# A two-layer hybrid diffusion backbone: output projection in pair steps, middle vectors in buffers of their own, gate pieces ahead of attention, y rests on VectorE

## What is computed

```python
for l in range(2):
    h = rmsnorm(x) * (1 + sc1) + sh1            # sc, sh, g come from silu(c) @ mod_w[l] + mod_b[l]
    ym = sigmoid(h @ w_mo) * head_norm(mlstm(h))          # 4 heads of 128, both directions
    ya = window_attention(rope(h @ w_aq), ...)            # 8 heads of 64, window 128, sink
    yr = silu(h @ w_rg) * head_norm(retention(h))         # 4 heads, values 256 wide, both directions
    y = (sigmoid(h @ w_gm) * (ym @ w_br_m) + sigmoid(h @ w_ga) * (ya @ w_br_a)
         + sigmoid(h @ w_gr) * (yr @ w_br_r)) @ w_out
    x = x + g1 * y
    h2 = rmsnorm(x) * (1 + sc2) + sh2
    x = x + g2 * conv_ffn(h2)                             # 2816 wide, gated, conv over 3 tokens
out = rmsnorm(x) * final_norm_w
```

## Time and profile before

| what | value |
|---|---|
| three runs | 3087.06, 3088.95, 3093.79 us; median 3088.95 us |
| the profiled execution's own time | 3092.63 us |
| its span from the first to the last instruction | 3090.8 us |
| TensorE busy | 2915.1 us, 94% of the span |
| granted TensorE clock, mean | 0.976 of full speed |
| VectorE, ScalarE, GpSimd busy | 37%, 32%, 39% |
| DMA | 249.8 MB, 81 GB/s over the span |

### The profile page before, as it was taken

One profiled execution on the slowest core, in us unless ns is written; L12 is line 12 of the kernel. 1 busy time (PEld: TensorE's weight loads), 2 busy tenths in 40 slices (PEclk: granted clock), 3 DMA queues, 4 the chain that ended last, 5 costly groups with the idle time before them and its releaser, 6 DMA issues. The chain is left out here.

```text
span 3090.8 us, 48199 instructions
## 1 busy us (share of the span) xinstructions
PE 2915.1 (94%) x19520; PEld 2586.9 (84%) x19520; DVE 1152.7 (37%) x2711; ACT 981.2 (32%) x1672; POOL 1216.5 (39%) x1078
## 2 busy tenths in 40 slices
PE   7999899999999997999999989989999989799998
PEld 5899878898888995888888779987898889788876
DVE  4545435423331023433333635424523320233345
ACT  4333225432322114322222333323532332332332
POOL 2333411153444423433443334341164455455554
PEclk9999999999999998999999999999999999899999
DMA  5111200022222125111111321120022322322222
GB/s 221 56 69 48 77 34 21 8 93 82 83 96 83 55 76 198 55 69 68 69 55 69 116 90 69 49 96 28 15 93 104 125 87 87 119 83 95 96 96 102
DMA packets 39385, 249.81 MB, mean 81 GB/s; under 512 B 4480, under 2 KB 4864, under 8 KB 13568
## 3 DMA queue, kind: packets, MB, share of 16 engines
q1 hardware_dynamic: 36288, 236.25, 21.5%
q10 hardware_dynamic: 2880, 10.49, 0.8%
HBM read 236.23 MB, written 10.49 MB: 80 GB/s over the span
## 5 line engine op out<-in xcount | busy, mean ns | idle before, releaser
L2090 POOL TENSOR_TENSOR w_rest<-raw,w_head 128x512 fp32r<-128x512 f32 (+1 forms) x642 | 842.0, 1344 | 991.8 <-ACT w_head L1193 982.0
L817 PE MATMUL psum_products<-w_head,h_head 128*128 128x256 f32 x2368 | 689.4, 291 | 0.0
L817 PE MATMUL psum_products<-w_rest,h_head 128*128 128x256 f32 x2368 | 666.2, 281 | 0.0
L817 PE MATMUL psum_products<-w_head,h_rest 128*128 128x256 f32 x2368 | 665.5, 281 | 0.0
L817 PE MATMUL psum_products<-h_head,w_head 128*128 128x512 f32 (+3 forms) x1696 | 600.1, 354 | 11.6 <-POOL w_rest L2090 8.6
L817 PE MATMUL psum_products<-h_head,w_rest 128*128 128x512 f32 (+3 forms) x1696 | 596.5, 352 | 0.0
L817 PE MATMUL psum_products<-h_rest,w_head 128*128 128x512 f32 (+3 forms) x1696 | 596.4, 352 | 0.0
L817 PEld LDWEIGHTS psum_products<-w_head,h_head 128*128 128x128 f32 x2368 | 454.0, 192 | 4.0 <-issue 1.4
L817 PEld LDWEIGHTS psum_products<-w_rest,h_head 128*128 128x128 f32 x2368 | 453.0, 191 | 1.3
L817 PEld LDWEIGHTS psum_products<-w_head,h_rest 128*128 128x128 f32 x2368 | 453.6, 192 | 0.0
L1193 ACT ACTIVATE w_head<-raw 128x2048 fp32r<-128x2048 f32 (+2 forms) x170 | 307.5, 1809 | 449.5 <-PE psum_products L817 392.7
(11 more groups left out here) (255 smaller groups left out, 3996.1 us busy)
## 6 DMA issues: line engine op xcount, KB each, us to landing
raw<-in_stream SPq DMA_DIRECT2D x192, 1024.0 KB, 4.8
raw<-in_stream SPq DMA_DIRECT2D x16, 512.0 KB, 3.3
residual<-stage ACTq DMA_DIRECT2D x16, 512.0 KB, 2.8
stage<-residual SPq DMA_DIRECT2D x14, 512.0 KB, 5.6
mods_b<-in_stream SPq DMA_DIRECT2D x5, 1024.0 KB, 24.1
mods_a<-in_stream SPq DMA_DIRECT2D x3, 1024.0 KB, 13.9
x_in<-in_x SPq DMA_DIRECT2D x4, 512.0 KB, 8.8
stage<-in_x SPq DMA_DIRECT2D x4, 512.0 KB, 5.9
```

What stands on the lines that cost most here:

```text
L817: return nc.tensor.matmul(o, a, b, start=start, stop=stop)
L2090: G.tensor_tensor(wl[:, s["sp"] % 2, a:b], place_of(s)[:, a:b], wh[:, s["sp"] % 2, a:b].bitcast(F32), ALU.subtract).then_inc(*ev.mark("poo ...
```

## The change

It has six parts.

1. **Output projection.** Of the four column blocks only 0 and 1 are done whole. Blocks 2 and 3 alternate pair by pair, and behind each such step but the first stands one tick of `norms`: (pair 0, block 2), (pair 0, block 3), tick 0, (pair 1, block 2), tick 1 and so on. The head of h is freed pair by pair (`h_free`) instead of with the whole slot (`w_free`).
2. **Middle vectors.** The eight vectors of layer 0's middle get four buffers of their own (`mods_mid`, in the arena over the MLP's rings), and stand behind the fifth tick: 6 pieces, tick 5, 6 pieces, tick 6, 4 pieces. SyncE issues their first four loads at the last `wout` block (`ahead = 6`).
3. **Gate pieces.** Four of the attention's gate pieces stand ahead of tick 0 of `attend`, behind the rotary steps; `attend` spreads four fewer.
4. **The end of the mLSTM.** In its last head two more vectors are taken: one more piece 0 behind each of the last ticks, and their pieces 1 behind `ysplit`.
5. **Retention.** Heads 2 and 3 take two vectors each instead of three.
6. **y rests.** The rest of yT in `ysplit` is made by VectorE instead of GpSimd.

```diff
@@ make_plan
+    def vectors(count, homes=False):
+
+        turn, mids = None, []
         for l, n in islice(modulation, count):
-            now = vector(l, n, cols("mod_w", l, n * COLS, splits=False))
+            s = cols("mod_w", l, n * COLS, splits=False, home=8 + len(mids) % 4 if homes else None)
+            if homes:
+                s["before"] = mids[-4] if len(mids) >= 4 else None
+                mids.append(s["n"])
+            now = vector(l, n, s)
...
             if hd + 1 == MH:
+                late = vectors(2)
+                pieces, fill = pieces + 2, chain(fill, islice(late, 2))
                 ticks("mtiles", count, fill, pieces, l=l, hd=hd, tiles=tiles)
                 continue
...
         step("ysplit", l=l, br="m", kt=4, tiles=tiles)
+        for _ in late:
+            pass
...
-        ticks("attend", AH * len(tiles) + 3, fill, 12 * len(pairs(ctx)), l=l,
+        for _ in islice(fill, 4):
+            pass
+        ticks("attend", AH * len(tiles) + 3, fill, 12 * len(pairs(ctx)) - 4, l=l,
...
-            more, last = vectors(3), len(tiles) + 1
-            more_now = 6 if hd + 1 < RH else 4
+            count_v = 3 if hd < 2 else 2
+            more, last = vectors(count_v), len(tiles) + 1
+            more_now = 2 * count_v if hd + 1 < RH else 2
...
-        for n in range(3):
+        for n in range(2):
             step("wout", cols("w_out", l, n * COLS), 3, l=l, gen=gen, n=n, ctx=ctx)
         step("affine", l=l, which=1)
-        wout, h_gen = cols("w_out", l, 3 * COLS), gen
+        wouts, h_gen = [cols("w_out", l, n * COLS) for n in (2, 3)], gen
...
-        for pair in pairs(ctx)[:-1]:
-            step("wout", wout, 1, l=l, gen=h_gen, n=3, ctx=ctx, pair=pair, part=pair, open=True)
-        ticks("norms", 2, stop=2, **mid)
-        step("wout", wout, 1, l=l, gen=h_gen, n=3, ctx=ctx, pair=2, part=2)
-        fill = vectors(2 * D // COLS) if ctx else iter(())
-        for k in range(2, len(tiles) + 2):
+        k = 0
+        for pair in pairs(ctx):
+            for i, n in enumerate((2, 3)):
+                step("wout", wouts[i], 1, l=l, gen=h_gen, n=n, ctx=ctx, pair=pair, part=pair,
+                     open=(pair, n) not in ((pairs(ctx)[0], 2), (2, 3)))
+                if pair != pairs(ctx)[0] or n == 3:
+                    step("norms", ticks=range(k, k + 1), **mid)
+                    k += 1
+        fill = vectors(2 * D // COLS, homes=True) if ctx else iter(())
+        for k in range(k, len(tiles) + 2):
+            for _ in islice(fill, 6 if k < len(tiles) + 1 else 4):
+                pass
             step("norms", ticks=range(k, k + 1), **mid)
-            for _ in islice(fill, 3):
-                pass
@@ backbone
+        home_mid = Region(8 * 1024 + 128)("mods_mid", [P, 4, SLOT])
...
                     ahead = 1 if kind == "split" else 3 if s["sp"] is not None else 2
+                    if kind == "wout" and st["n"] == 3 and st["ctx"]:
+                        ahead = 6
...
                             if use == "mid":
+                                act.wait_ge(*ev.at("h_free", st["l"], t // 2))
...
+                elif kind == "ysplit":
+                    for t in st["tiles"]:
+                        ts = slice(t * P, (t + 1) * P)
+                        dve.wait_ge(*ev.at("yh", l, st["br"], t))
+                        V.tensor_tensor(yl[:, 0:st["kt"], ts], yT[:, 0:st["kt"], ts],
+                                        yh[:, 0:st["kt"], ts].bitcast(F32), ALU.subtract).then_inc(
+                            *ev.mark("dve", "ysplit", l, st["br"], t))
```

More of the change, by code:

```diff
@@ L117, in slot @@
     def slot(l, blocks, kt=KD, splits=True, home=None):
-        s = dict(n=len(stream), l=l, blocks=blocks, kt=kt, cols=sum(b[1] for b in blocks[2]), sp=None, home=home)
+        s = dict(n=len(stream), l=l, blocks=blocks, kt=kt, cols=sum(b[1] for b in blocks[2]), sp=None, home=home,
+                 before=None)
         if home is None:
@@ L163, in vector @@
         return turn
-    def vectors(count):
-        turn = None
+    def vectors(count, homes=False):
+        turn, mids = None, []
         for l, n in islice(modulation, count):
-            now = vector(l, n, cols("mod_w", l, n * COLS, splits=False))
+            s = cols("mod_w", l, n * COLS, splits=False, home=8 + len(mids) % 4 if homes else None)
[3 more added lines that the diff above has]
+            now = vector(l, n, s)
             yield
@@ L651, in place_of @@
                 return raw[:, s["r"] % 2, 0:n]
+            if s["home"] >= 8:
+                return home_mid[:, s["home"] - 8, 0:n]
             return home_a[:, s["home"], 0:n] if s["home"] < 3 else home_b[:, s["home"] - 3, 0:n]
@@ L751, in load @@
                 s = STREAM[i]
-                if s["home"] is None and s["before"] is not None:
+                if s["before"] is not None:
                     sp.wait_ge(*ev.at("raw_free", s["before"]))
@@ L999, in _ @@
                     part_b(st, 0, COLS)
+                    if kind == "wout" and st["n"] == 3:
+                        ev.now["h_free", l, st["pair"]] = {"pe": ev.count["pe"]}
                 elif kind == "branch":
@@ L1246, in _ @@
                         if k >= 2 and use != "last":
-                            if k == 2 and st["h_slot"] is not None:
+                            t = st["tiles"][k - 2]
+                            if use == "mid":
+                                act.wait_ge(*ev.at("h_free", st["l"], t // 2))
+                            elif k == 2 and st["h_slot"] is not None:
                                 act.wait_ge(*ev.at("w_free", st["h_slot"]))
-                            t = st["tiles"][k - 2]
                             act.wait_ge(*ev.at("hf", st["gen"], k - 2))
```

7 lines of the change are left out of this document (removed).

## The result

| | before | after | ratio (95% interval) |
|---|---|---|---|
| median of the runs, first timing | 3088.38 us | 3039.59 us | 0.9831 (0.9805 to 0.9857) |
| the same two kernels, second timing | 3101.19 us | 3037.18 us | 0.9793 (0.9776 to 0.9811) |
| the same two kernels, third timing | 3098.98 us | 3043.63 us | 0.9822 (0.9798 to 0.9846) |
| span of the profiled executions | 3090.8 us | 3037.6, 3034.2, 3044.2 us | |

A forecast was written before the change was run, and what follows sets the result against it. TensorE, busy 94% of the span, was taken as the bound, with its waits and low clock. Six terms summed to 63.8 us: 3092.6 to 3028.8 profiled, 3025 for the median, range 3009 to 3050.

The forecast's parts named there:

- Term 1: Layer 0's middle: pair steps cover tick chains and vector slots come ahead; 87.0 to 63.3 us, 23.7 saved, bounds 20 to 30.
- Term 2: Layer 1's middle: the 5.41 wait goes, the 6.42 wait stays, only earlier; 5.5 us saved, bounds 3 and 8.
- Term 3: Four gate pieces ahead of attention fill 4.78 of waiting and restore 1.6 of clock; 12.8 us saved in two layers.
- Term 4: Retention's branch: y rests on VectorE remove waits of 3.50 and 4.08 and half clock; 11.0 us saved, bounds 5 and 13.
- the serial case: Retention's branch, at worst: y rests and weights' rest one behind the other, done 3.2 us early in layer 0, 0.4 in layer 1.
- Term 5: End of the mLSTM: shorter chain to the branch product, two added vectors hidden; 4.5 us saved, bounds 0 and 6.
- Term 6: Retention: four vectors fewer in two layers at 1.58 each; 6.3 us saved if hidden where they went, else 0.
- Attention shortened: Against the rival that attention's ticks are chains and do not shorten: 12.8 us lost, 3038; chance alone 0.13.
- The middle of layer 0 was not held up: Against the rival that GpSimd or vector slots hold it up: gain 12, not 23.7, 3037; chance 0.17, with loads held up.
- The slower case: Both middles: if a tick's chain exceeds its 5.65 step, TensorE waits at ten places at half clock; 3100 us, chance 0.03.
- No part failed to do what it says: Against the rival of vector loads late in SyncE's order: middle's 7.48 back, 15 us, 3040; chance 0.17, with middle held up.
- the waits for `xs` would fall from seven to two or three: Sign in the changed profile: that fall in TensorE's `xs` waits, none over 1 us in layer 0's pair-step ticks.

The follow-up runs named there:

- the other spread: Changed kernel with retention-head pieces dealt out two a tick until none is left, in place of evenly: 3033.16 us, ratio 0.9780 to the kernel before.
- mid_order_old: Changed kernel with both middles in the order before, the vectors still in buffers of their own: 3048.99 us, ratio 0.9859 to the kernel before.
- gates_in: Changed kernel with the four gate pieces put back among attention's ticks: 3055.21 us, ratio 0.9872 to the kernel before.
- Ret3: Changed kernel with three vectors in each retention head again and none added at the mLSTM's end: 3045.26 us, ratio 0.9813 to the kernel before.

## Why the prediction was right or wrong

Gains in the stretches, before (one trace) against the mean of the three traces of the changed kernel:

| term | forecast | found | by itself |
|---|---|---|---|
| 1. middle, layer 0 | 23.7 | 22.1 (on the mean of seven) | order 9.5, buffers 17.8 |
| 2. middle, layer 1 | 5.5 | 3.5 | order 0.8 |
| 3. attention | 12.8 | 8.0 + 9.3 = 17.3 | 15.1 (14.1 on twelve) |
| 4. y rests at the retention | 11.0 | 5.8 + 4.9 = 10.7 | 10.2 |
| 5. end of the mLSTM | 4.5 | 0.8 + 1.1 = 1.9 | |
| 6. retention heads 2, 3 | 6.3 | -1.1 + 0.0 (0.1 + 0.2 on ten) | 10 to 11 more with the other spread |
| sum | 63.8 | 54.4 | |

The spans differ by 52.1 (3090.8 against 3038.7 on the mean of three); in these three traces alone term 1 is 23.4 and the sum 55.7, so 3.6 us were lost elsewhere. The forecast's sum was too high by 9.4 in these stretches, and that is terms 5 and 6 above all (10.8 forecast, 0.8 found), then term 2 and term 1; that term 3 made up for 4.5 of it was luck. How near the size came is a matter of the timing too: the sum's 63.8 stands beside 48.8 at the first, and 64.0 and 55.4 at the others.

- **Term 1 was right** in its steps: 61.8, 62.2 and 66.8 us for 63.3, no wait over 1 us for `xs` at the pair steps, no slot waited for, and the one wait put down at 3.3, GpSimd with the first MLP slot's rests in hand, stands there as 3.40 (the last row below). It left out one that the new order brings in both layers, 1.53 ahead of block 3's first pair, whose weights' rest is not made yet. The group `const,vec` was misread: its 5.34 ran at clock 0.70 and not at half, and at full it takes 3.82, not 2.7, so that the 4.2 put down held by luck.

```profile
1128.07 0.38 PE L838 MATMUL psum_products<-w_head,h_head 128*128 128x256 f32 x1 [1.53 <-POOL w_rest L2122]
...
1168.56 0.75 PE L951 MATMUL psum_mixers<-const,xs 128*128 128x128 f32 x4 [3.40 <-ACT xs L1282]
```

- **Term 2 was too large.** The step that failed is "so this stays, only earlier". The 5.41 went and the 6.42 became 9.10. First, the 6.42 was not GpSimd's four pieces, as the forecast read it. Those ended at 2686.23, and GpSimd then waited 2.35 for the tick's squares; what held the tick was its sum, 2.35 long behind the last eviction, and an inverse root that took 1.40 beside VectorE's next sum:

```profile
2684.24 0.69 DVE L1663 TENSOR_TENSOR acc<-psum_products,gate_b 128x512 f32<-128x512 f32 x1 [5.99 <-PE psum_products L817]
2684.97 2.35 DVE L1625 TENSOR_TENSOR stage<-stage,acc 128x1024 f32<-128x1024 f32 x1
```

```profile
2688.59 0.19 POOL L2117 TENSOR_SCALAR small<-small 128x1 f32<-128x1 f32 x1 [2.35 <-ACT xs L1235]
2688.86 1.40 POOL L2120 TENSOR_TENSOR small<-small,const 128x1 f32<-128x1 f32 x1
```

In the changed kernel the statistic follows the four pieces by 0.08, so now they bound the tick. Second, they came hardly earlier: they began 28.6 us into the window before (2681.17 - 2652.6) and 27.2 after (2631.43 - 2604.2), while TensorE was done with the second tick's transposes 6.0 earlier (from the windows' starts, 32.5 and 26.5). The head of that slot stands behind the second tick in ScalarE's list, in both kernels, and that tick has a pair step more ahead of it now. The weight buffer was free by then: VectorE evicts the last product with block 2 from 2622.92 on, and ScalarE starts the head 6.5 later, without a wait, right behind the tick's `hf`:

```profile
2628.06 1.49 ACT L1293 ACTIVATE hf<-psum_mixers,aff 128x128 f32<-128x128 f32 x4
2629.43 1.92 ACT L1216 ACTIVATE w_head<-raw 128x2048 fp32r<-128x2048 f32 x1
```

All waits over 0.3 us of this stretch are 17.3 in mid_order_old and 15.8 in the changed kernel. Of the 3.5 found only that 0.8 is the order's. Mid_order_old has the order of before, and still takes 78.3 against its 81.0: the same 336 matmuls of the output projection took 38.3 us there and 39.8 before, both at clock 1.00, and the clock behind the same wait of 5.41 was 0.88 and 0.72. So the other 2.7 lies in the one trace of the kernel before, and is not a gain of the change.
- **Term 3 was too small** by 1.3 to 4.5, by which of its sizes one takes. The wait and the half clock are as summed: from the first product to the end of `attend` it is 7.4 shorter in layer 0, 5.65 + 1.6 being 7.25 (8.8 in layer 1). The late start was put at 0.9 and is 0.5 in layer 0. What was left out is the gate step ahead of the branch: in layer 0 it ran at clock 0.92 in 18.9 us before, and at 1.00 in 17.5 to 18.2 in the changed kernel. In gates_in it is back at 19.1 and 0.92, so in layer 0 it belongs to the pieces; in layer 1 gates_in ran it at 1.00 too.
- **Term 4 was right**, in its sum and in its margin: both waits went, 10.7 for 11.0. Of the serial case by which it was bounded the rows show the order, but not that the port made it. By the rule of the Trainium skill, "SBUF — State Buffer", section "Who interferes with whom", which made the two take turns, the trace agrees in layer 1 only in so far as they did not overlap, which the end of the weights' head explains as well; the contention itself is in the middle, where a sum beside GpSimd's rests took 2.17 and four rests 6.20, and 1.23 and 5.03 apart.
- **Term 5 was wrong in its chain and its clock**, not in its vectors. It put the chain to the branch at 1.2 shorter in layer 0 and 1.3 in layer 1, with 0.3 and 1.7 of clock behind. Ret3, without the two vectors, shows the y rests alone: the wait of 2.93 only fell to 2.31 in both layers, and the 4 us behind it ran at 0.62 and 0.60, where the kernel before had 1.00 and 0.57. So the chain gave 0.6, and no clock came back:

```profile
343.73 0.55 PE L834 MATMUL psum_products<-w_head,y_head 128*128 128x256 f32 x1 [2.31 <-DVE y_rest L1946]
```

The two vectors are hidden as forecast: 62.3 and 44.3 with them, 62.5 and 44.4 without.
- **Term 6 was wrong.** It went by the price of an instruction (1.58 a vector) in a place bound by a chain. The forecast had the condition in words ("if they are hidden where they went") and never asked what a vector had been hiding where it came from. It was cover: with 12 pieces on 7 ticks the second tick of layer 0's head 2 was left with 12 matmuls ahead of GpSimd's scores. In the four heads the longest waits for scores, 1.44, 2.83, 1.02 and 2.38 before, are 2.86, 2.51, 2.40 and 3.49 after, 3.6 us more for 6.3 taken out, and the clock fell behind them (0.95 in head 2 of layer 0). The row was to be had: before the change TensorE already waited 8.2 us for `r_s` from GpSimd, and the forecast did not count with it:

```profile
PE psum_mixers L817 <- POOL r_s L2162: 8.2, 5, 2.8
```

- **The rivals.** Attention shortened. The middle of layer 0 was not held up. The slower case fell with the pair steps, whose ticks show no wait for `xs` over 0.4 us. No part failed to do what it says. Of the signs named, that the waits for `xs` would fall from seven to two or three did not come: there are still seven, 21.7 us in all.

## What to carry to other kernels

A filler that is taken out of a chain-bound stretch is worth nothing until one has looked at what it covered and how an even spread rounds what is left; deal pieces out where the wait is. When a chain is moved up, look for work that keeps its place in another engine's list and has the next link behind it (here a split of weights, which stayed behind the second tick). Read from the rows which of two things ended a wait; both were near the 6.42. And compare by stretches that two programs share: single spans of one program differed by 10 us here, more than most parts of the change.

## What was not expected of the hardware

**The same program has two paces of matmuls at full clock.** One stretch, 60 us of the retention's branch in layer 0, in the changed kernel, in its second and in its third trace:

```profile
1000.00:1060.00 60.00, 60.00 (x532) 60.00 (x531) 3.44 (x5) 9.72 (x10) 24.13 (x19) 1.00 0.20 71
```

```profile
1000.00:1060.00 60.00, 60.00 (x512) 60.00 (x511) 3.44 (x5) 10.00 (x10) 21.63 (x17) 1.00 0.19 69
```

```profile
1000.00:1060.00 60.00, 60.00 (x532) 60.00 (x531) 4.12 (x6) 8.65 (x8) 27.21 (x22) 1.00 0.20 71
```

TensorE never waits and the granted clock is 1.00 in all three, but 532 matmuls are done in the one and 512 in the other: 112.8 and 117.2 ns each. A stretch keeps its pace for tens of microseconds, and the whole branch takes 114.4 or 118.9 us by it. Over the branch alone that is 4.5 us. Other stretches have the same two paces at clock 1.00 in every trace: the last three blocks of the retention's branch take 97.9 or 101.8 us in layer 0 and 65.3 or 67.8 in layer 1, attention's branch 32.8 or 34.1 in layer 0, and the changed kernel's three traces have both of each. What sets the pace stays open.

**The clock behind the same wait differs from run to run.** The stretch with the 3.40 wait in layer 0's middle and the one behind it, in the second trace, then in the third:

```profile
1161.70:1169.20 7.50, 3.13 (x43) 1.88 (x40) 3.60 (x9) 2.57 (x5) 7.33 (x7) 1.00 0.98 344
1169.20:1183.40 14.20, 14.04 (x137) 10.96 (x137) 7.12 (x21) 9.51 (x18) 8.94 (x6) 0.88 0.81 338
```

```profile
1164.40:1171.90 7.50, 3.12 (x42) 1.88 (x40) 3.60 (x9) 2.57 (x5) 7.33 (x7) 1.00 0.97 340
1171.90:1190.70 18.80, 18.66 (x136) 13.81 (x137) 7.20 (x21) 9.51 (x18) 8.92 (x6) 0.64 0.61 257
```

The same work with the same idle time ahead, and then a clock of 0.88 or of 0.64, 14.2 or 18.8 us: 4.6 us that nothing in the program decides. A wait that is left is so worth more than its length, but only in some runs; a forecast should carry it as a range, not as a sum.
